# Gate and up weights of an expert in one load and one product, down weights by column quarters

## What is computed

```python
gate = ...   # (tokens, 64), 8 entries of a row not zero
a = silu(einsum('td,edf->tef', x, w_gate)) * einsum('td,edf->tef', x, w_up)   # w_gate, w_up: 64 x 1024 x 256
routed = einsum('tef,efd->td', a * gate[..., None], w_down)                   # w_down: 64 x 256 x 1024
shared = (silu(x @ ws_gate) * (x @ ws_up)) @ ws_down
y = routed + shared
```

## Time and profile before

| | us |
|---|---|
| median of 3 runs (lowest, highest) | 640.89 (640.74, 641.63) |
| profiled execution, its own time | 641.84 |
| its span, first to last instruction | 640.2 |
| TensorE busy | 580.9 (91%) |
| VectorE, ScalarE, GpSimd busy | 211.8, 167.8, 32.8 |
| moved by DMA | 252.55 MB, 394 GB/s mean |

### The profile page before, as it was taken

How to read it: one execution, slowest core, us unless ns; L and a number is a source line. 1 busy time by engine, 2 the same in 40 slices (tenths; PEclk the granted TensorE clock), 3 DMA queues, 4 the chain that set the end, 5 groups by cost and what they waited for, 6 DMA issues and landing times.

```text
span 640.2 us, 11142 instructions
## 1 busy us (share of the span) xinstructions
PE 580.9 (91%) x4568; PEld 404.6 (63%) x4568; DVE 211.8 (33%) x479; ACT 167.8 (26%) x308; POOL 32.8 (5%) x78
## 2 busy tenths in 40 slices
PE   0799999999999999989999999596999999998776
PEld 0488777788867676657575767363567676765353
DVE  0297868687822212011222122020121212122104
ACT  3182727672622121202121212010112121212010
POOL 1340210011100000000000000000000000000002
PEclk9989999999999999999999999797999999999779
DMA  9998699979989999999999999999999999999995
GB/s 354 411 373 321 215 366 389 431 300 422 402 359 389 387 425 418 421 420 420 422 420 421 420 422 418 422 420 421 421 421 420 421 422 419 421 420 421 421 391 173
DMA packets 37078, 252.55 MB, mean 394 GB/s; under 512 B 4872, under 2 KB 7568, under 8 KB 9888
## 3 DMA queue, kind: packets, MB, share of 16 engines
q1 hardware_dynamic: 34512, 246.90, 94.2%
q0 software_dynamic: 1840, 4.21, 2.0%
q10 hardware_dynamic: 672, 0.69, 0.3%
HBM read 250.06 MB, written 1.72 MB: 393 GB/s over the span
## 4 chain that ended last, share of the span: by engine, by line
PE 68%; DMA 19%; SPq 6%; ACT 3%; DVE 2%; issue 1%; POOL 0%; POOLq 0%; DVEq 0%; ACTq 0%
PE bank L1276 22%; PE bank L1351 12%; DMA ring<-in_w_up 9%; PE bank L1247 6%; PE bank L1293 6%; DMA ring<-in_w_down 6%; DMA ring<-in_w_mod 3%; SPq L562 3%; PE bank L846 3%; PE bank L888 2%; PE bank L896 2%; PE bank L892 2%; SPq L633 2%; DMA ring<-in_w_in 1%; PE bank L1009 1%; PE bank L1210 1%
## 5 line engine op out<-in xcount | busy, mean ns | idle before, releaser
L1276 PE MATMUL bank<-ring,xe 128*64 128x256 f32 (+1 forms) x1520 | 176.9, 402 | 10.5 <-DMA ring<-in_w_up 8.9
L1276 PEld LDWEIGHTS bank<-ring,xe 128*64 128x64 f32 (+1 forms) x1520 | 110.7, 133 | 50.7 <-issue 24.8
L1351 PE MATMUL bank<-ring,actT 128*64 128x512 f32 (+1 forms) x384 | 86.6, 627 | 6.4 <-DMA ring<-in_w_down 4.8
L2322 DVE TENSOR_TENSOR act_e<-bank,sil 128x256 f32<-128x256 f32 x26 | 11.1, 425 | 188.4 <-ACT sil L1737 188.4
L2336 DVE SCALAR_TENSOR_TENSOR ylo<-bank,gslot,yhi 128x512 fp32r<-128x512 f32 x50 | 37.5, 751 | 83.4 <-ACT yhi L1750 83.4
L1750 ACT ACTIVATE yhi<-bank,gslot 128x512 fp32r<-128x512 f32 x50 | 34.4, 688 | 115.9 <-PE bank L1351 115.9
L1737 ACT ACTIVATE sil<-bank 128x256 f32<-128x256 f32 x26 | 10.0, 385 | 192.6 <-PE bank L1276 192.6
L1247 PE MATMUL bank<-pone,hhi 128*128 128x256 f32 x200 | 50.0, 288 | 0.0
L1351 PEld LDWEIGHTS bank<-ring,actT 128*64 128x64 f32 (+1 forms) x384 | 25.4, 132 | 37.2 <-issue 37.0
L1247 PE MATMUL bank<-pone,hlo 128*128 128x256 f32 x200 | 48.9, 282 | 0.0
L1276 PE MATMUL bank<-rows_tile,xe 128*64 128x256 f32 (+1 forms) x128 | 34.6, 432 | 9.8 <-DMA ring<-in_w_up 6.3
(11 more groups left out here) (388 smaller groups left out, 844.6 us busy)
## 6 DMA issues: line engine op xcount, KB each, us to landing
ring<-in_w_gate SPq DMA_DIRECT2D x49, 1024.0 KB, 25.1
ring<-in_w_down SPq DMA_DIRECT2D x48, 1024.0 KB, 26.3
ring<-in_w_up SPq DMA_DIRECT2D x46, 1024.0 KB, 26.2
ring<-in_w_mod SPq DMA_DIRECT2D x12, 2048.0 KB, 11.7
ring<-in_w_in SPq DMA_DIRECT2D x5, 2048.0 KB, 14.5
gb<-in_w_up SPq DMA_DIRECT2D x5, 1024.0 KB, 22.9
spare<-in_w_gate SPq DMA_DIRECT2D x4, 1024.0 KB, 27.2
ring<-in_w_out SPq DMA_DIRECT2D x2, 2048.0 KB, 14.6
```

The source lines that it names most:

```text
L1276: ins = mm(bank[6][j * w:(j + 1) * w, part * FE:(part + 1) * FE], xe[:, k, slots], weights[:, k, :], start=(k == 0), stop=(k == KD - 1))
L1351: ins = mm(bank[4 + h][j * w:(j + 1) * w, :], actT[:, f, j * w:(j + 1) * w], weights[:, f, 512 * h:512 * h + 512], start=(f == 0), stop=(f ...
```

## The change

1. `TWO_TILE_UNITS` are units 4 to 14. There the gate and the up tile of an expert are loaded by one DMA of 2048 KB into two neighbouring ring places, 16 KB in a row for each partition. For that the host lays gate and up of an expert side by side in one array. In all other units gate and up are loaded apart, as before, out of rows of that array.
2. In these units `gate_up` makes one product of 512 columns for each k (256 of gate from the first place, 256 of up from the second) in place of two of 256. It waits for the expert's one load; `gate_used` is not raised there, and the places are released by `e_filled`.
3. The places are handed out otherwise: a two-tile load takes the ring pair (2m, 2m+1) that was used longest ago; the down tiles of units 4 to 14 go only to spare, gb, xn and rows_tile; single tiles of the other units go to the oldest free place, in unit 15 without gb and xn.
4. The down weights lie in four column quarters in memory and in the tile (quarter, row half j, 256 columns), so that a part of columns is one run for each partition: 4 KB and 2 KB rows in the loads of the end, where it was two of 2 KB and of 1 KB. A down product of 512 columns reads two runs of 256.

```diff
+TWO_TILE_UNITS = range(4, UNITS - 1)
+def loads_of(unit):
+
+    if unit not in TWO_TILE_UNITS:
+        return [(i, i) for i in range(NTILE)]
+    if unit in QUAD_UNITS:
+        return [(j, 4 + j) for j in range(4)] + [(8 + j, 8 + j) for j in range(4)]
+    return [(6 * par + a, 6 * par + b) for par in range(2) for a, b in ((0, 2), (1, 3), (4, 4), (5, 5))]
...
+            if lo != hi:
+                sets = [[2 * m, 2 * m + 1] for m in range(NTILE // 2)]
+            elif unit in TWO_TILE_UNITS:
+                sets = [[p] for p in (SPARE, OVER_GB, OVER_XN, OVER_ROWS)]
+            else:
+                sets = [[p] for p in held if p not in lent]
+            left, at = min((max(held[p] for p in s), s) for s in sets)
...
+            def load_two_tiles(unit, i, e):
+                at = PLACE[unit, i]
+                sp.dma_start(ring[:, at * EW:(at + 2) * EW], gate_up_dram[e]).then_inc(tile_loaded[at], 16)
...
-            released(REPLACES[UNITS * NTILE - 1])
+            released(*max(REPLACES[UNITS - 1, i] for i in range(NTILE - NSLOT, NTILE)))
...
+                if not again and unit_of(kind, par, unit) in TWO_TILE_UNITS:
+                    for j in range(kind):
+                        weights_ready(pe, kind, par, 0, j, unit, again)
+                    for k in range(KD):
+                        for j in range(kind):
+                            at = PLACE[unit_of(kind, par, unit), tile_of(kind, par, 0, j)]
+                            weights = ring[:, at * EW:(at + 2) * EW].rearrange("p (a k f) -> p k a f", a=2, k=KD)
+                            slots = slice(par * P + j * w, par * P + (j + 1) * w)
+                            ins = mm(bank[6][j * w:(j + 1) * w, :], xe[:, k, slots], weights[:, k, :, :],
+                                     start=(k == 0), stop=(k == KD - 1))
+                    ins.then_inc(e_filled, 1)
+                    return
...
+    w_down = np.asarray(inputs["w_down"])[0].reshape(NE, P, JF, D // FE, FE)
+    inputs["w_down"] = w_down.transpose(0, 1, 3, 2, 4).reshape(NE, P, EW)
+    parts = [np.asarray(inputs.pop(name))[0].reshape(NE, P, EW) for name in ("w_gate", "w_up")]
+    inputs["w_gate_up"] = np.concatenate(parts, axis=2)
```

More of the change, by code:

```diff
@@ L524, in weights_of @@
             i = tile_of(kind, par, part, j)
-            return tile(i if again else PLACE[unit_of(kind, par, unit) * NTILE + i])
+            return tile(i if again else PLACE[unit_of(kind, par, unit), i])
         def weights_ready(pe, kind, par, part, j, unit, again):
@@ L628, in released, with load_columns @@
                     after(FIRST_STEP[unit] + i // 6, i % 6 // 2)
-            def load_columns(g, e, i):
+            def load_columns(j, e, i):
                 w = FINAL[i]
-                ins = sp.dma_start(tile(PLACE[g]).rearrange("p (j n) -> p j n", j=JF)[:, :, w],
-                                   down_dram[e].rearrange("p (j n) -> p j n", j=JF)[:, :, w])
-                ins.then_inc(last_columns[i] if i < 2 else tile_loaded[PLACE[g]], 16)
+                at = PLACE[UNITS - 1, NTILE - NSLOT + j]
+                v = slice(JF * w.start, JF * w.stop)
+                ins = sp.dma_start(tile(at)[:, v], down_dram[e][:, v])
+                ins.then_inc(last_columns[i] if i < 2 else tile_loaded[at], 16)
             def refill(unit, experts, first=0, end=NTILE):
-                for i in range(first, end):
-                    g = unit * NTILE + i
-                    if REPLACES[g] is None:
+                for i, other in loads_of(unit):
+                    if not first <= i < end:
+                        continue
+                    if REPLACES[unit, i] is None:
                         sp.wait_ge(sorted_filled, 1)
@@ L644, in refill @@
                     else:
-                        released(REPLACES[g])
-                    load_tile(g, experts[i % 4 if unit in QUAD_UNITS else 2 * (i // 6) + i % 2])
+                        released(*REPLACES[unit, i])
+                    e = experts[i % 4 if unit in QUAD_UNITS else 2 * (i // 6) + i % 2]
+                    if other == i:
+                        load_tile(unit, i, e)
+                    else:
+                        load_two_tiles(unit, i, e)
             def experts_of(unit):
@@ L1349, in down @@
                         for j in range(kind):
-                            weights = weights_of(kind, par, 2, j, unit, again).rearrange("p (j n) -> p j n", j=JF)
                             ins = mm(bank[4 + h][j * w:(j + 1) * w, :], actT[:, f, j * w:(j + 1) * w],
-                                     weights[:, f, 512 * h:512 * h + 512], start=(f == 0), stop=(f == JF - 1))
+                                     down_columns(weights_of(kind, par, 2, j, unit, again), f, slice(512 * h, 512 * h + 512)),
+                                     start=(f == 0), stop=(f == JF - 1))
                     ins.then_inc(y_filled, 1)
```

75 lines of the change are left out of this document (42 added, 33 removed).

## The result

The changed kernel takes 646.73 us (median of 8 runs), the kernel before, timed beside it, 641.88: a ratio of 1.0075, 95% interval 1.0056 to 1.0095, so it is slower by 4.8 us (3.6 to 6.1). Forecast were +0.8% and 5.0 us on the profiled span of 640.2; the profiled execution after has a span of 643.2 and took 644.72, as much as the quickest of its eight runs, so the two profiled spans are only 3.0 us apart and the ratio of the medians is what counts.

The account below looks back on a forecast made before the run. The weight stream from about 225 us to the last column load was taken as DMA-bound, TensorE close behind. Bytes -4.3, tail -0.35 and stall +9.6 gave +5.0 us: 645.9 us on the median (+0.8%), range 641.5 to 651.0.

Parts of the forecast that it names:

- The term that decided: DMA queue runs dry at 458.2 us until step 15's down product releases places at 465.1: stall 9.6 us.
- Rivals A: The DMA queue does not run dry behind step 15: 636.2 us; chance 0.09.
- B: The queue runs dry for only 3.4 to 5.9 us: within 0.2% of before; chance 0.06.
- D: Reading two places as one operand is slower in gate/up products: 653 us at 25% slower; chance 0.04.
- Cheaper bytes: Gate/up loads of units 4 to 14: 16 KB rows save 0.098 us for each of 44 experts, 4.3 us.
- Rival C: 16 KB rows are cut up or no faster in this stream, nothing saved: 650.2 us; chance 0.10.
- Products: Two-expert gate/up as 32 matmuls of 512 columns, not 64 of 256: no gain and no loss.
- Tail: Column loads at the end have rows of double length and are quicker: -0.35 us.
- Nothing won back: After the stall the kernel stays DMA-bound, TensorE with 4.6 us to spare, so no lost time returns.
- The sum: Whole kernel: -4.3 - 0.35 + 9.6 = +5.0 us on the profiled span of 640.2, giving 645.2.

Follow-up runs that it names:

- pairs first: Changed kernel with unit 10's four gate/up pairs all issued before its four down tiles; 637.99 us, ratio 0.9929 to the kernel before.
- both cures: Changed kernel with unit 10's four pairs ahead of its down tiles and the shared expert's down product behind step 15's own; 636.67 us, ratio 0.9910.
- the places alone: Changed kernel with each pair as two 1024 KB loads and the product in two parts, leaving places and column quarters; 653.07 us, ratio 1.0167.
- loads apart: Changed kernel with each two-tile load made as two loads of 1024 KB with 8 KB rows; 649.17 us, ratio 1.0110.
- the run of the quarters: Kernel before with only the down weights laid out by column quarters, down products reading two runs of 256; 641.52 us, ratio 0.9992.

## Why the prediction was right, point by point

**The term that decided (9.6 us).** Right in place and mechanism; that the size was met to 0.1 us is partly luck. The hole was forecast behind step 15, from 458.2 to a release at 465.1; measured, the last pair landed at 455.9 and the release came at 461.8. The pieces: from the end of gate/up to the end of down 17.0 us (forecast 16.9), first landing 4.9 us after issue (5.0), 9.6 us of lost DMA time in all by the parts (9.6). But the hole itself was 8.5 us, and the other 1.2 are the pair behind it that took 6.09 us, of which the prediction has nothing. One piece was off by as much the other way: step 15's gate/up took 8.48 us, not 9.8, since the granted clock was 0.83 on average over it, where 0.50 for nearly the whole product was assumed from the earlier trace rows. (The upper bound of the stall adds up to 12.6, not 12.7.) The window of that product:

```profile
436.30:444.80 8.50, 8.45 (x65) 2.42 (x65) 0.00 (x0) 0.00 (x0) 0.00 (x0) 0.83 1.03 429
```

All stood some 2 to 3 us earlier than forecast, which is what this execution was ahead of the one before when the last tile of unit 1 landed (table above).

By the ratios, taking the hole away gave 9.4 us (pairs first) and 10.6 (both cures), and the places alone cost 11.2. Rivals A and B fall, and so does D: gate/up groups of two-expert steps take 6.87 us with two places read as one operand, and 6.91 in two parts.

**Cheaper bytes (4.3 us).** Mechanism right, size too large: 0.068 us a pair, not 0.098, so 3.0 us; the runs gave 2.2 and 3.1. It was not the row of 16 KB that misled: on the first DMA engine one pair follows the other by 4.89 to 4.90 us (428 GB/s) in units 4 to 9, where 4.88 was forecast. Two single tiles of the kernel before take 4.97 there (2.484 each), where 421 GB/s made them 4.98. The saving is the small difference of two large numbers, and 0.01 to 0.02 us on each of them, both in the same direction, made 0.07 into 0.098. Rival C falls.

**Products (0).** Wrong. Three pairs of kernels differ in nothing else: 2.5 us (changed kernel; 0.8 to 4.2), 2.1 (both cures; 0.2 to 3.9), 3.7 (the places alone against loads apart; 1.6 to 5.7), all in favour of the one product. The sentence that fails is "Halved weight loads give nothing, since they lie beside the matmuls". It asks only where the TensorE's time goes, and leaves out that instructions themselves come by the DMA, which is the bound here. That instruction packets cost time was shown (GpSimd's 6000 instructions, 10.2 us). That the five packets are the whole of the 2 to 4 us was not: on average over the engines they take some 0.3 to 0.5 us, and between the last tiles of units 1 and 15 the profiled executions with the product in two parts were 2.4 us longer in the first pair, 1.4 shorter in the second and 1.8 longer in the third, and the kernels of these pairs were 1.7, 4.1 and -1.0 us apart near 83 us already, long before the first product that differs (278 us). So single executions scatter by as much as the term. What share of it the packets have is open, and with it the cause of this term.

**Tail (-0.35).** Within what the run of the quarters could tell: -0.5 us, interval -1.4 to +0.4.

**Nothing won back.** Right. The twice-made shared product cost its 6.9 us (6.7 by the spans), and the TensorE did wait again before step 24: in the chain after, the last pair of unit 14 lands at 593.6 (forecast near 595), and the product follows it:

```profile
567.39 26.17 DMA ring<-in_w_gate_up
...
593.70 10.05 PE bank L1314 x64
```

**The sum.** Forecast -4.3, 0, -0.35, +9.6 = +5.0. Measured in parts: loads -2.2 to -3.1, product -2.1 to -3.7, quarters -0.5, places +9.4 to +11.2; together +4.8. The bytes were put too large by some 1.3 us and the products missed by 2 or more, which partly cancelled: that the sum came out to 0.2 us is luck. That the sign and the range held is not, since both hang on the hole, and that was sized from rows.

## What to carry to other kernels

When a queue is issued in order and buffers are dedicated to kinds of data, count at every place where a consumer comes late how much may still be issued ahead of the first blocked load: here 20 us of tiles stood against a release 25.6 us away, and putting two loads whose places were free ahead of the one whose place was not turned +0.8% into -0.7%. In a kernel at DMA share 1.0 count instructions as traffic as well, since they hold up single DMA engines and a transfer waits for the slowest. Larger transfers pay little once the queue is deep (0.07 us less for 2 MB in one load than in two), so they are not worth a place scheme that can run dry.

## What was not expected of the hardware

Instructions of an idle engine cost time: 6000 waits on GpSimd, 23 packets of 8 KB at 0.31 us, made a DMA-bound kernel 10.2 us slower, by putting one of the 16 DMA engines up to 12.7 us behind the first, in steps of 0.6 to 0.9 us a packet. In the kernel before, too, this spread grows from 3.0 to 7.2 us over the stream; a hole in the stream closes it (3.5 to 1.7 us in the changed kernel), since the engine that is behind loses less of it than the others: in unit 10 the last parts lost 9.6 us, the first parts 11.4.
